# Front of a decoder step: half blocks of shift and scale, eight groups of two input chunks, rows of x first in the queue

## The reference

```python
def adaln_mod(c, w, b):
    m = jax.nn.silu(c) @ w + b
    return jnp.split(m[:, None, :], 3, axis=-1)

shp, scp, gtp = adaln_mod(c_prompt, ada_w[layer], ada_b[layer])     # and the same for the 8 samples
hp = rmsnorm(xp, norm_g[layer]) * (1.0 + scp) + shp
...
u_a, v_a, z_a, q_b, k_b, v_b, z_b = jnp.split(h @ w_in, idx, axis=-1)
```

## Time and profile before

| | us |
|---|---|
| median of 3 runs | 1221.91 |
| lowest and highest | 1221.26, 1224.97 |
| span of the profiled execution | 1224.2 |
| first product of the projection (L308) | 49.19 |
| TensorE busy, share of the span | 96% |
| DMA over the span | 325.13 MB, 266 GB/s |

### The profile page before, as it was taken

The page is one execution under the profiler, slowest core; times in us unless marked ns, Lnnn a source line. Parts: engine busy times, 40 slices in busy tenths (PEclk is TensorE's granted clock), DMA queues, the critical chain, the costliest instruction groups (busy, mean ns, idle before and its releaser), DMA issues.

```text
span 1224.2 us, 27727 instructions
## 1 busy us (share of the span) xinstructions
PE 1176.7 (96%) x11376; PEld 1090.0 (89%) x11376; DVE 703.6 (57%) x1323; ACT 568.9 (46%) x724; POOL 331.9 (27%) x207
## 2 busy tenths in 40 slices
PE   5899999999999999999999999899999989999997
PEld 2699999999988887787879999899999989999997
DVE  1655555555544645733544546578999896583112
ACT  3323323233344353422333236577767766575443
POOL 0000000010000003200000002567766679605773
PEclk9999999999999999999999999999999999999999
DMA  9989999999898887899999899485858445455542
GB/s 332 309 273 338 320 297 316 372 376 373 285 332 299 270 292 254 259 376 344 317 375 366 295 325 260 157 279 171 283 155 286 138 138 182 143 173 158 163 148 94
DMA packets 236978, 325.13 MB, mean 266 GB/s; under 512 B 12429, under 2 KB 152525, under 8 KB 236429
## 3 DMA queue, kind: packets, MB, share of 16 engines
q1 hardware_dynamic: 233472, 312.78, 76.3%
q0 software_dynamic: 2192, 7.79, 2.2%
q10 hardware_dynamic: 1188, 2.79, 0.8%
HBM read 317.96 MB, written 7.06 MB: 265 GB/s over the span
## 4 chain that ended last, share of the span: by engine, by line
PE 85%; DVE 8%; DMA 2%; ACT 2%; issue 2%; SPq 1%; POOL 0%; DVEq 0%; ACTq 0%
PE PS L308 22%; PE PS L311 21%; PE PS L312 21%; PE PS L401 6%; PE PS L1009 4%; DVE PS L1785 3%; PE PS L1036 3%; PE PS L1267 2%; DMA XR<-in_ada_w 2%; DVE WLO L302 1%; PE PS L537 1%; SPq L385 1%; PE PS L427 1%; ACT WHI L297 1%; ACT ACTS L650 0%
## 5 line engine op out<-in xcount | busy, mean ns | idle before, releaser
L308 PE MATMUL PS<-HH,WHI 128*128 128x288 f32 x2176 | 662.7, 305 | 18.3 <-DVE HL L486 5.2
L312 PE MATMUL PS<-HH,WLO 128*128 128x288 f32 x2176 | 643.5, 296 | 0.0
L311 PE MATMUL PS<-HL,WHI 128*128 128x288 f32 x2176 | 643.2, 296 | 0.0
L297 ACT ACTIVATE WHI<-WRAW 128x1024 fp32r<-128x1024 f32 x272 | 283.8, 1055 | 381.5 <-PE PS L312 320.8
L308 PEld LDWEIGHTS PS<-HH,WHI 128*128 128x128 f32 x2176 | 410.8, 189 | 31.6 <-issue 23.9
L311 PEld LDWEIGHTS PS<-HL,WHI 128*128 128x128 f32 x2176 | 411.0, 189 | 0.0
L312 PEld LDWEIGHTS PS<-HH,WLO 128*128 128x128 f32 x2176 | 410.4, 189 | 0.0
L302 POOL TENSOR_TENSOR WLO<-WRAW,WHI 128x1024 fp32r<-128x1024 f32 x117 | 281.4, 2428 | 193.5 <-ACT WHI L297 193.0
L302 DVE TENSOR_TENSOR WLO<-WRAW,WHI 128x1024 fp32r<-128x1024 f32 x155 | 191.0, 1234 | 156.5 <-ACT WHI L297 155.8
L1785 DVE SCALAR_TENSOR_TENSOR PS<-ACTS,CWT,PS 128x288 f32<-128x288 f32 x448 | 192.5, 514 | 4.2 <-ACT PS L1770 3.4
L1022 DVE COPY ACTS<-PS 128x512 f32<-128x512 f32 x64 | 44.0, 688 | 70.2 <-PE PS L1009 70.2
(11 more groups left out here) (284 smaller groups left out, 721.2 us busy)
## 6 DMA issues: line engine op xcount, KB each, us to landing
XR<-in_ada_w SPq DMA_DIRECT2D x192, 512.0 KB, 8.5
WRAW<-in_ab_w_in SPq DMA_DIRECT2D x112, 512.0 KB, 7.4
WRAW<-in_c_w_in SPq DMA_DIRECT2D x96, 512.0 KB, 3.6
XR<-in_cache_b_k SPq DMA_DIRECT2D x128, 256.0 KB, 5.3
XR<-in_cache_b_v SPq DMA_DIRECT2D x128, 256.0 KB, 5.9
WRAW<-in_ab_w_out SPq DMA_DIRECT2D x32, 512.0 KB, 9.0
WRAW<-in_c_w_out SPq DMA_DIRECT2D x32, 512.0 KB, 3.5
ACTS<-in_x_prompt ACTq DMA_DIRECT2D x2, 1024.0 KB, 10.9
```

The source lines that it names most:

```text
L297: act.activation(WHI[:, i % 4], WRAW[:, i % 4], ACT.Copy).then_inc(w_hi, 1)
L308: first = pe.matmul(out, whi, HH[:, k, :], start=start, stop=False)
L311: pe.matmul(out, whi, HL[:, k, :], start=False, stop=False)
L312: return pe.matmul(out, wlo, HH[:, k, :], start=False, stop=stop)
```

## The change

The rows of x, the small vectors, the convolution weights and the page table move to the head of SyncE's queue; ScalarE's queue keeps only the condition, now as 128 and 16 rows of 128 numbers. Each conditioning block 0 to 7 holds 256 columns of shift and the same 256 of scale, so that one block serves two input chunks. Block 0 alone is summed before the products, in quarters between the transposes of x, and in the same form as all others; `first_sum` and its three helpers are gone. Shift and scale bias get their + 1 once. A weight chunk of the q, k, v projection is 2 input chunks x 512 columns, so there are 8 groups of 6 chunks; a chunk makes two bank pairs (`s_half` for the first, `w_used` for the second) and 96 of them are emptied: the first 12 by ScalarE (`part_first`), 84 by VectorE (`part_add`). GpSimd makes the low parts of chunks 6 to 47. The sums' places move, sum 11 by one chunk. The convolution weights are loaded as 124 rows and turned by 4 transposes in the start. The scaling of q is done in one go at chunk 46.

```diff
-JO = NQKV + 16 + 16 - P_AB
+NPART = 2 * NQKV
+JO = NPART + 16 + 16 - P_AB
+QKV_ORDER = (4, 5, 6, 7, 0, 1, 2, 3, 8, 9, 10, 11)
...
         def w_load(sp, i):
...
+            if i < NQKV:
+                k, col = 2 * (i // 6), 256 * (12 + QKV_ORDER[2 * (i % 6)])
+                sp.dma_start(halves(WRAW, c), win_v[:, k:k + 2, col:col + 512]).then_inc(w_raw[c], 16)
...
         def load_ada(sp, x, a, c):
...
+            if a < 8:
+                for part_of in range(2):
+                    col = D * part_of + 256 * a
+                    sp.dma_start(XR[:, c, :].rearrange("p (k n) -> p k n", k=4)[:, :, 256 * part_of:256 * part_of + 256],
+                                 ada_v[0, :, 4 * c:4 * c + 4, col:col + 256]).then_inc(x_rdy[c], 16)
+                return
...
+        def small_loads(sp):
...
+            sp.dma_start(VROWS2, ada_b.rearrange("l (k p) -> (l k) p", p=P)).then_inc(s_vec, 16)
+            sp.dma_start(CWROW, c_conv_w[0].rearrange("w (k p) -> (w k) p", p=P).rearrange("(t r) p -> r t p", t=4)
+                         ).then_inc(s_cw, 16)
...
+            ada_quarter(pe, 0, 0, M0, 2)
+            pe.wait_ge(s_cw, 16)
+            for t in range(4):
+                last = pe.transpose(PS[:, M1, 124 * t:124 * t + 124], CWROW[:, t, :], IDENT[0:124, 0:124])
+            last.then_inc(s_cwt, 1)
+            ada_quarter(pe, 0, 0, M0, 3)
...
             lo(pool, 0)
+            for i in range(6, NQKV):
+                lo(pool, i)
...
-        SUM_AT = {3: 2, 8: 3, 13: 4, 19: 5, 25: 6, 31: 7, 37: 8, 41: 9, 45: 10}
+        SUM_AT = {4: 1, 9: 2, 14: 3, 19: 4, 24: 5, 29: 6, 34: 7, 38: 8, 42: 9, 46: 10}
...
         def part_products(pe, i):
...
+            g, c = i // 6, i % 4
+            whi, wlo = halves(WHI, c), halves(WLO, c)
+            pe.wait_ge(w_lo[c], i // 4 + 1)
+            for pair in range(2):
+                q = 2 * i + pair
+                if q >= 3:
+                    pe.wait_ge(acc_free, q - 2 if q < SINGLE + 2 else q - 1)
+                for kk in range(2):
+                    k = 2 * g + kk
+                    if i % 6 == 0:
+                        pe.wait_ge(s_hl, k + 1)
+                    for n in range(2):
+                        out = PS[:, part_set(q)[n], 0:R]
+                        at = slice((2 * pair + n) * P, (2 * pair + n + 1) * P)
+                        pe.matmul(out, whi[:, kk, at], HH[:, k, :], start=kk == 0, stop=False)
+                        pe.matmul(out, whi[:, kk, at], HL[:, k, :], start=False, stop=False)
+                        last = pe.matmul(out, wlo[:, kk, at], HH[:, k, :], start=False, stop=kk == 1)
+                last.then_inc((s_half, w_used)[pair], 1)
...
         def qkv_act(act):
             for i in range(NQKV):
...
+                if i < 6:
+                    part_first(act, 2 * i)
+                    hi(act, i + 2)
+                    part_first(act, 2 * i + 1)
+                if i >= 5:
+                    for n in {5: (8,), 6: (9, 10), 7: (11,)}.get(i, (i + 4,)):
+                        hi(act, n)
+                if i in SUM_AT and SUM_AT[i] < 8:
+                    modulate(act, SUM_AT[i])
...
         def prompt_pe(pe):
...
-            ada_sum(pe, 11, 11, M1)
             rest_chunk(pe, 2)
+            ada_sum(pe, 11, 11, M1)
...
         @block.sync
         def _(sp):
+            sp.dma_start(XROW[0], xp_v[0:P]).then_inc(s_rows[0], 16)
+            sp.dma_start(XROW[1], xp_v[P:2 * P]).then_inc(s_rows[1], 16)
+            sp.dma_start(XROW[2], xs_v).then_inc(s_rows[2], 16)
+            small_loads(sp)
+            w_load(sp, 0)
             load_ada4(sp, 0, 0)
-            w_load(sp, 0)
-            load_ada4(sp, 1, 1)
-            i = 1
-            for a, upto in ((2, 5), (3, 11), (4, 16), (5, 21), (6, 27), (7, 33), (8, 39), (9, 45), (10, 49), (11, 53),
+            w_load(sp, 1)
+            w_load(sp, 2)
+            i = 3
+            for a, upto in ((1, 3), (2, 9), (3, 14), (4, 19), (5, 24), (6, 29), (7, 34), (8, 39), (9, 43), (10, 47), (11, 51),
                             (12, 57), (13, 60), (14, 63), (15, 66)):
                 while i < upto:
                     w_load(sp, i)
                     i += 1
-                load_ada4(sp, a, a)
+                for c in range(4):
+                    load_ada(sp, a, a, c)
+                    if a < 11 and c < 3:
+                        w_load(sp, i)
+                        i += 1
```

More of the change, by code:

```diff
@@ L416, in ada_home @@
             dve.wait_ge(ada_tr, a + 1)
+            if a < 8:
+                dst, bias = (t.rearrange("p (t c) r -> p t c r", t=2)[:, :, 2 * a:2 * a + 2] for t in
+                             (ADA[:, 0:32, :], bc(V_ADAB[:, 0:32].unsqueeze(2), [P, 32, NC9])))
+                src = ADAT.rearrange("p (t c r) -> p t c r", t=2, c=2)[:, :, :, 0:NC9]
+                dve.tensor_tensor(dst, src, bias, ALU.add).then_inc(ada_done, 1)
+                return
+            b, layer = (a, 0) if a < 12 else (a - 12, 1)
             bias = V_ADAB[:, 48 * layer + 4 * b:48 * layer + 4 * b + 4]
@@ L541, in start_pe @@
         def start_pe(pe):
-            pe.wait_ge(s_ident, 3)
+            pe.wait_ge(s_ident, 2)
             pe.wait_ge(s_silu, 1)
-            for k in range(KC):
-                last = pe.transpose(PS[:, M3, k * 32:(k + 1) * 32], CROW[:, k * P:(k + 1) * P], IDENT[0:32, 0:32])
-            last.then_inc(s_setup_pe, 1)
-            pe.wait_ge(s_setup_cp, 1)
-            def between(c):
-                if c == 2:
-                    for t in range(3):
-                        pe.wait_ge(s_rows[t], 16)
-                    for k in range(4):
-                        x_turn(pe, k)
-            first_sum(pe, 0, 0, M0, between)
-            for k in range(4, 8):
+            pe.transpose(PS[:, M3, 0:P], CONDS, IDENT[:])
+            pe.transpose(PS[:, M3, P:P + KC], CONDP, IDENT[0:KC, 0:KC]).then_inc(s_setup_pe, 1)
+            for t in range(3):
+                pe.wait_ge(s_rows[t], 16)
+            for k in range(8):
+                x_turn(pe, k)
+            pe.wait_ge(s_setup_cp, 1)
+            ada_quarter(pe, 0, 0, M0, 0)
+            for k in range(8, 13):
+                x_turn(pe, k)
+            ada_quarter(pe, 0, 0, M0, 1)
+            for k in range(13, KC):
                 x_turn(pe, k)
@@ L561, in start_pe @@
             pe.transpose(PS[:, M2, 112:208], VROWS2, IDENT[0:96, 0:96]).then_inc(s_setup_pe, 1)
[L562 to L564 removed]
             pe.wait_ge(s_consts, 1)
[L566 to L567 removed]
+            pe.transpose(PS[:, M2, 256:384], ROWSEED, IDENT[:]).then_inc(s_setup_pe, 1)
             pe.wait_ge(x_diag, 1)
@@ L594, in start_dve @@
             dve.reciprocal(RT[:, 0:3], RT[:, 0:3]).then_inc(s_stat, 1)
-            for k in range(8, KC):
+            for k in range(12, KC):
                 x_copy(dve, k)
@@ L727, in qkv_pe, with part_first, part_add @@
+        def part_first(act, q):
+            act.wait_ge((s_half, w_used)[q % 2], q // 2 + 1)
+            dst, src = part_view(q)
+            act.activation(dst, src, ACT.Copy).then_inc(acc_free, 1)
+        def part_add(dve, q):
+            dve.wait_ge((s_half, w_used)[q % 2], q // 2 + 1)
+            if q % PAIRS_QKV == 0:
+                dve.wait_ge(acc_free, q)
+            dst, src = part_view(q)
+            dve.tensor_tensor(dst, src, dst, ALU.add).then_inc(acc_free, 1)
         def qkv_pe(pe):
@@ L729, in qkv_pe @@
                 part_products(pe, i)
-                if i == 4:
-                    pe.wait_ge(s_cw, 16)
-                    pe.wait_ge(acc_free, 3)
-                    for w in range(CW):
-                        last = pe.transpose(PS[:, M3, w * KC:(w + 1) * KC], CWROW[:, w * P:(w + 1) * P], IDENT[0:KC, 0:KC])
-                    last.then_inc(s_cwt, 1)
-                    pe.wait_ge(s_setup_cp, 4)
                 if i >= 45:
-                    pe.wait_ge(acc_free, 44)
+                    pe.wait_ge(acc_free, SINGLE + 4)
                     row_fill(pe, 2 * (i - 45))
```

277 lines of the change are left out of this document (110 added, 167 removed).

## The result

| | median us | lowest to highest | runs |
|---|---|---|---|
| before | 1223.44 | 1221.26 to 1225.42 | 4 |
| changed | 1238.42 | 1235.65 to 1242.04 | 4 |

The changed kernel takes 1.0132 of the time of the kernel before, with a 95% interval of 1.0096 to 1.0168. The forecast was 1211.6 us. So the change makes the kernel slower by 1.3 to 1.7%, and the forecast had the wrong sign.

What follows compares the result with a forecast made beforehand. TensorE's products were taken to set the pace (busy 96%). Start -10.4, projection -4.9 and new waits +5.0 summed to -10.3 us, from 1221.9 to 1211.6 us; 8-in-10 range 1204.5 to 1221.0.

Steps and rivals of the forecast that it cites:

- Start to first product: From kernel start to TensorE's first product: 38.8 us instead of 49.19, 10.4 us earlier.
- The term for the convolution weights: In the start's loads: 512-byte pieces land slowly, adding 3.0 us before the first quarter, between 0 and 9.9.
- rival A: In the start, convolution weights on a quarter of the engines: first quarter 6.2 us later, time 1217.8 us; chance 0.20.
- A difference of -10.3 carries over: Whole kernel: profiled execution 1224.2 us, 2.3 over the median 1221.9; -10.3 us applied to the median gives 1211.6.
- First product to end of the projection: First projection: block 1's sum +3.6, small turns, copy wait and slow stretch -4.4, bank wait -1.7, HL waits -2.4; -4.9 us.
- what is doubled and moved: In the projection: 48 more VectorE emptyings (36 us) cost nothing; splits moved to GpSimd add 0.8 us at the beginning.
- Later in the queue: SyncE's later loads: 1.0 us for three four-chunk periods and 3.2 us more wait in sum 12; +5.0 with GpSimd's 0.8.
- Chunk 7 and GpSimd: At the projection's beginning: GpSimd's split of chunk 7 ends 0.8 us after TensorE wants it, between 0 and 2.4.
- B: Rival for the projection's periods: DMA becomes the bound, a period takes 22.3 us, time 1226.9 us; chance 0.12.
- C: Rival for the whole projection: no wait comes back, small loads cost nothing, time 1205.3 us; chance 0.20.
- C's other sign: In the start: a first product before 38 us would show that no wait comes back.

Runs made afterwards that it cites:

- b2_queue51: Kernel before with weight chunks up to 51, not 53, ahead of block 11's transfers on SyncE; ratio 1.0036 to the kernel before.
- b1_pool_lo: Kernel before with weight splits 4 to 47 moved from VectorE to GpSimd; ratio 1.0071 to the kernel before.
- k4: Kernel before, unchanged, run once more for a second profile of its start; time 1227.09 us.
- m2_gate3: e1 with a GpSimd wait for the sum's HL parts, set before the split three chunks ahead of the sum's; ratio 0.9963 to the kernel before.
- e1: Changed kernel with weight chunks up to 53, not 51, ahead of block 11's transfers on SyncE; ratio 1.0129 to the kernel before.
- g2: Changed kernel with GpSimd's first split behind each of sums 1 to 7 waiting for that sum's HL parts; ratio 1.0065 to the kernel before.
- g1: e1 with GpSimd's first split behind each of sums 1 to 7 waiting for that sum's HL parts; ratio 0.9981 to the kernel before.
- n2_after_again: Changed kernel, unaltered, compared once more on another chip; ratio 1.017 to the kernel before.
- k3: g3 with the convolution weights' load behind block 0's quarters on SyncE, not ahead of them; ratio 0.9971 to the kernel before.
- g3: e1 with GpSimd's weight splits on VectorE, mostly three chunks ahead, between a chunk's two emptyings; ratio 0.9998 to the kernel before.
- k1: g3 with 31 filler matmuls in TensorE's three waits of the start; ratio 1.0005 to the kernel before.
- k2: Kernel before with 36 filler matmuls ahead of its first transposes; ratio 1.002 to the kernel before.
- n1: m2_gate3 with late convolution weights, 24 filler matmuls, and those weights' turns behind the last quarter, their copy behind the scaled x; ratio 0.9917 to the kernel before.

## Why the prediction was wrong

**Start to first product: the sum right, in part by luck.** 38.63 us against 38.8. In nine profiled executions with this start it came at 36.3 to 40.6, 38.9 in the mean. Two misses cancel: the first quarter landed at 19.55 us and not at 18.1, and from its first matmul to the end of the sum it took 16.3 us and not 18.2, since the last quarter and part of the turns ran at the higher level (1.36 us for that quarter, 1.94 for the first). The term for the convolution weights (+3.0) was near in size: taken away, they gave back 4.4 us, so rival A's 9.2 is excluded. It was wrong in kind: the forecast had slow pieces landing, and 3.5 of the 4.4 us were SyncE's late issue.

**The comparison it was made with: half right.** "A difference of -10.3 carries over" to the median rests on one profile of the kernel before, with a first product at 49.19. A time here is 1.7 us above the span of its execution in nearly every run that has both (2.4 at most), so that profile stands near 1225.9 us (an estimate), 4.0 over the median and not 2.3. b2_queue51 has the same start and reached its first product at 41.62. Its turns and quarters ran at the other level; TensorE of b2_queue51:

```profile
20.27 1.07 PE L427 MATMUL PS<-XR,CT 128*32 128x512 f32 x8 [1.27 <-DMA XR<-in_ada_w]
21.26 2.24 PE L537 MATMUL PS<-IDENT,ACTS 128*128 128x128 f32 x12
```

The earlier trace rows has 1.93 us for that quarter, and the twelve turns behind it took 3.51 us there. The granted clock printed 1.00 from 20 to 40 us in both. In b1_pool_lo, which has this start too and its first product at 49.58, it printed 0.50:

```profile
30.00:40.00 10.00, 10.00 (x38) 6.16 (x38) 6.23 (x20) 1.63 (x3) 2.35 (x1) 0.50 1.07 368
```

The kernel before has the same TensorE time and count in that window (10.00, x38) with 1.00 printed, so the printed clock did not show the low level there. The 119 times of the kernel before in the five comparisons lie in two heaps, 66 below 1222.5 us with most from 1216 to 1220, and 53 above with most from 1224 to 1228. The distance fits the 7.6 us, and the two profiles of this kernel (the one of the front and k4) have the late start and a time in the upper heap. That the lower heap is the early start is not shown: no profile of the unchanged kernel fell into it. If it is, the start's gain is 3 us in half of the runs and 10 in the others, and the forecast was some 4 us too good on this alone.

**First product to end of the projection: wrong in what it left out.** -4.9 was right in each item that the profile can show: the waits for a bank of the earlier trace rows, for CWT and the four for HL are gone. m2_gate3, which repairs the two faults below and nothing else, takes 293.4 us where the terms gave 291.1. The changed kernel's own profile adds up the same way: 291.0 - 4.9, then 2.6 for chunk 7, sum 8 and sum 12, then 9.6 and 5.1 (waits and clock) at sums 2, 4 and 6, 8.5 and 2.7 at the row fills, and 2.0 for the late weight chunk. That is 316.6 where 317.2 was measured; the two clock terms are estimates, half of each low stretch.

**The step that failed** is the one on what is doubled and moved: "It costs nothing" for the emptyings, and "the exposed VectorE operations would be the HL pairs, 0.9 us a period, so that by this rule nothing would be added to the sum". In the changed kernel the HL pairs of the sums were not hit at all (in b1 two HL parts were). The bias, the gain and the two modulations are tensor_tensors with both inputs in SBUF as well, and I had read them only as 0.2 us in the start's sum. Each can stand for what is left of a split, up to 2.4 us, and two splits in a row catch two of them. They stand directly ahead of the HL parts and, in VectorE's queue, of the emptyings. This cost 9.6 us of waits and about 5 of clock in the profile. By m2 against e1 it is 10.3 us, by g2 against the changed kernel 12.4, and 8 to 13 by the ratios of those two. The Trainium skill's rule ("SBUF — State Buffer", Who interferes with whom), that two inputs in SBUF contend with a GpSimd instruction that reads SBUF and that the one which issues first holds the shared ports for its whole instruction, agrees with this trace: 1.94 to 2.39 us where 0.18 to 0.22 is normal, each ending with GpSimd's split. I asked only what it does to the HL pairs, and not what it does to the shorter operations ahead of them.

**Later in the queue: the wrong neighbour.** I counted what stands behind the quarters of periods with four chunks (1.0 us; sum 8 waited 1.46) and behind sum 12 (3.2 us more; it waited 1.64 for its load where it had been 0.88, so 0.8 more, and 1.6 in m2 too). I did not follow the number (11, 51), which puts weight chunks 51 and 52 behind block 11, to ScalarE's list, where the rounding of 51 stands ahead of a row copy. That is 13.5 us by e1's profile and 10 us by g1 against g2, and b2_queue51 shows it in the kernel before. Nor did I follow the weight chunk that lands late ahead of 241.5 us; it cost 2.0 us here and 1.8 in m2, and no run takes it apart from the rest.

**Chunk 7 and GpSimd:** a wait of 0.4 us against 0.8.

**Rivals.** A: landing 1.45 us later than forecast, not 6.2. B, the only slower one, had the right sign by another mechanism: the five-chunk periods without a late emptying took 19.8 us as forecast (20.4 the first, with chunk 7) and no sum from 3 to 7 waited for XR, so DMA is not the bound there; the others took 24.6 to 25.0. C had under 1 us for sum 12 and the forecast about 4; 1.6 came. C's other sign, a first product before 38 us, was not there (38.63; 36.83 in n2_after_again).

## What to carry to other kernels

When work moves to GpSimd, list every VectorE operation with two SBUF inputs that can lie beside it, the shortest first, and price each at the length of GpSimd's instruction and not of its own; then read what stands behind it in VectorE's queue. A wait on GpSimd until the short chain is through added no wait of TensorE for a split here (0.4 us with it and without) and gave back about 10 us. Follow each load that changes places in a queue to the engine that consumes it and to whatever stands behind that step. And take more than one profile before a start at a low clock is entered in a sum.

## What the runs showed of the hardware

- In the sums of the changed kernel, all six VectorE operations with both inputs in SBUF that began while a GpSimd split had 0.5 us or more to run stood until it ended. In all runs together: 128x36 in up to 2.46 us and not 0.20, 128x1152 in up to 3.56 and not 1.35 (b1), and one in SBUF with a single tensor input (L638) 2.40 and not 0.18. The emptyings, with one input in a bank, were never lengthened (29 of 84 beside a split, 0.76 us). At 1124 us two HL parts kept their 0.47 us and the split beside them took 3.37 us and not 2.40.
- A load of 496 pieces of 512 bytes (254 KB, 124 partitions) held up what was queued behind it by 4.4 us (k3 against g3), 3.5 of them at the issue; the next issue on that queue took 3.4 us and not 0.4 (0.29 in k3).
- The start ran at either level from execution to execution with the same instructions (first product 41.6 or 49.2 to 50.1 us). The granted clock printed 1.00 from 20 to 40 us in one early start and in two late ones and 0.50 from 30 us in another late one (b1); the durations told them apart. Matmuls put ahead of a wait of 3 to 4 us did not keep the level behind it (k1, k2); where no wait of the start was over 1.3 us behind them (n1) the level held.
